# Expert slots of 160 rows in place of 128: a tail of 32 rows in float32 on four column strips

## What is computed

```python
moe = jnp.zeros_like(t)
for e in range(N_EXPERTS):          # 16
    he = jax.nn.silu(t @ w_gate[e]) * (t @ w_up[e])      # (1024, 512)
    moe = moe + gates[:, e:e + 1] * (he @ w_down[e])     # gates is 0 but for two experts a token
h = h + moe.reshape(B, S, D)
```

## Time and profile before

| | before |
|---|---|
| median of 3 runs | 1485.0 us (1484.18 to 1487.67) |
| span of the profiled execution | 1482.1 us |
| TensorE busy | 1413.0 us, 95% of the span |
| VectorE busy | 972.7 us, 66% |
| ScalarE busy | 856.3 us, 58% |
| chain that ended last | TensorE 74%, DMA 9%, VectorE 8%, ScalarE 6% |

### The profile page before, as it was taken

How to read it: one execution, slowest core, us unless ns; L and a number is a source line. 1 busy time by engine, 2 the same in 40 slices (tenths; PEclk the granted TensorE clock), 3 DMA queues, 4 the chain that set the end, 5 groups by cost and what they waited for, 6 DMA issues and landing times.

```text
span 1482.1 us, 21096 instructions
## 1 busy us (share of the span) xinstructions
PE 1413.0 (95%) x7429; PEld 1082.9 (73%) x7429; DVE 972.7 (66%) x1763; ACT 856.3 (58%) x1553; POOL 140.1 (9%) x205
## 2 busy tenths in 40 slices
PE   7999999999999999999999999978999999999996
PEld 5888999544445545468878887767788888888885
DVE  5513116367658876757763343378889899898887
ACT  6321467366656666653253333344678888878776
POOL 1000000122300200000000000001111111221211
PEclk9999999999999999999999999997999999999998
DMA  6231124420020000021120011246997666666694
GB/s 228 66 112 41 61 93 169 180 103 1 1 114 1 1 29 30 30 99 43 43 114 29 29 44 43 69 144 241 352 367 215 211 216 213 221 211 215 220 367 135
DMA packets 89397, 189.01 MB, mean 128 GB/s; under 512 B 14314, under 2 KB 24554, under 8 KB 88563
## 3 DMA queue, kind: packets, MB, share of 16 engines
q1 hardware_dynamic: 80050, 166.11, 31.5%
q0 software_dynamic: 7200, 22.03, 5.8%
q10 hardware_dynamic: 2080, 0.01, 0.1%
HBM read 218.54 MB, written 28.31 MB: 167 GB/s over the span
## 4 chain that ended last, share of the span: by engine, by line
PE 74%; DMA 9%; DVE 8%; ACT 6%; issue 3%; POOL 0%; DVEq 0%; ACTq 0%; SPq 0%; POOLq 0%
PE psum L2075 28%; PE psum L2323 17%; DMA up_stage<-in_w_up 8%; PE psum L2059 8%; PE psum L2218 7%; PE psum L2241 5%; PE psum L2200 4%; PE psum L2052 3%; DVE up_rest L1686 3%; DVE gate_rest L1686 1%; PE psum L2485 1%; ACT gate_high L1229 1%; ACT arena L1369 1%; ACT up_high L1229 1%; ACT arena L1204 1%
## 5 line engine op out<-in xcount | busy, mean ns | idle before, releaser
L898 ACT ACTIVATE arena<-psum 128x512 f32<-128x512 f32 (+3 forms) x195 | 85.7, 494 | 83.0 <-PE psum L2241 45.8
L1686 DVE TENSOR_TENSOR down_rest<-down_stage,down_high 128x1024 fp32r<-128x1024 f32 x96 | 115.0, 1219 | 25.4 <-ACT down_high L1229 25.3
L1686 DVE TENSOR_TENSOR up_rest<-up_stage,up_high 128x1024 fp32r<-128x1024 f32 x100 | 117.0, 1219 | 15.5 <-ACT up_high L1229 15.1
L2218 PE MATMUL psum<-arena 64*128 64x512 f32 (+7 forms) x384 | 115.9, 519 | 6.2 <-ACT arena L1185 4.1
L1571 DVE TENSOR_TENSOR_SCAN arena<-arena,singles 128x768 f32<-128x768 f32 (+7 forms) x64 | 86.4, 1364 | 53.7 <-POOL arena L786 47.5
L2059 PE MATMUL psum<-arena 128*128 128x512 f32 (+2 forms) x352 | 118.0, 487 | 0.8 <-DVE arena L1552 0.8
L1686 DVE TENSOR_TENSOR gate_rest<-gate_stage,gate_high 128x1024 fp32r<-128x1024 f32 x100 | 115.8, 1217 | 1.4 <-ACT gate_high L1229 1.3
L2075 PE MATMUL psum<-up_high,rows_high 128*128 128x256 f32 x384 | 110.2, 287 | 6.5 <-DVE up_rest L1686 6.1
L1229 ACT ACTIVATE up_high<-up_stage 128x1024 fp32r<-128x1024 f32 x100 | 100.3, 1056 | 23.9 <-DMA up_stage<-in_w_up 23.9
L2075 PE MATMUL psum<-up_rest,rows_high 128*128 128x256 f32 x384 | 108.6, 283 | 0.0
L2075 PE MATMUL psum<-up_high,rows_rest 128*128 128x256 f32 x384 | 108.6, 283 | 0.0
(11 more groups left out here) (417 smaller groups left out, 3535.2 us busy)
## 6 DMA issues: line engine op xcount, KB each, us to landing
gate_stage<-in_w_gate SPq DMA_DIRECT2D x25, 2048.0 KB
up_stage<-in_w_up SPq DMA_DIRECT2D x25, 2048.0 KB
down_stage<-in_w_down SPq DMA_DIRECT2D x24, 2048.0 KB
arena<-in_x SPq DMA_DIRECT2D x16, 512.0 KB, 3.7
arena<-in_w_mkv SPq DMA_DIRECT2D x8, 1024.0 KB, 6.3
arena<-in_w_in SPq DMA_DIRECT2D x4, 1024.0 KB, 10.9
arena<-in_w_mo SPq DMA_DIRECT2D x4, 1024.0 KB, 6.5
mv_times_w_mo_spill<-arena SPq DMA_DIRECT2D x8, 512.0 KB, 3.1
```

The lines of the kernel that those rows point to most:

```text
L898: do(act.activation(dst, src, ACT.Copy), s_te["act"])
L1686: ins = dve.tensor_tensor(split[part][1][:, k, :], stage[part][:, k, :], split[part][0][:, k, :].bitcast(F32), ALU.subtract)
L2218: mm = pe.matmul(scores_of(kind, n)[:, at:end], lhs, rhs(at, end), start=True, stop=True)
```

## The change

A slot now holds 160 rows of an expert: 128 as before and a **tail** of 32. The tail's rows are gathered and added on their own (`fetch_tail`, `add_tail`): the 32 rows of 1024 values are laid on 128 partitions as four pieces of 256. The tail's products are plain float32, not split, and read the weights from the stage itself. Each product of 32 rows is made four times side by side, on four strips of 32 output partitions of TensorE, each strip with another quarter of the columns (`tail_rows_by`, `tail_down`). In the queue they stand behind the main products: gate's tail behind up, up's tail behind the hidden transpositions, down's tail behind down, at the very end of the slot. Since they read the stages, `next_weights` waits for them too. Up is made in one piece of 512 columns, and the hidden values in one piece instead of two halves. The places in the table become rank + (256 - 160) x (rank // 160) + 256 x the slot.

```diff
-SLOTS = (2 * SEQ) // P + NE
+TAIL = 32
+STRIPS = P // TAIL
+ROOM = P + TAIL
+PIECE = DM // STRIPS
+SLOTS = (2 * SEQ) // ROOM + NE + 2
...
-            def next_weights(part, rests_done, e, new):
+            def next_weights(part, rests_done, tail_made, e, new):
+                if part == 1:
+                    sp.wait_ge(s_ua, tail_made)
                 sp.wait_ge(s_lo[part], rests_done)
+                if part != 1:
+                    sp.wait_ge((s_gf, s_ua, s_y)[part], tail_made)
                 load(e, part, new > 0)
...
                 fetch(idx[:, 0:1])
-                pool.wait_ge(s_yo, 2 * s + 2)
+                fetch_tail(idx[:, 2:3])
+                pool.wait_ge(s_yo, 3 * s + 2)
                 pool.sem_inc(s_go, 1)
                 add_rows()
-                pool.wait_ge(s_ya, 16 * s + 16)
+                pool.wait_ge(s_yo, 3 * s + 3)
+                pool.sem_inc(s_go, 1)
+                add_tail()
+                pool.wait_ge(s_ya, 32 * s + 32)
...
-                act.wait_ge(s_gf, s + 1)
+                act.wait_ge(s_gf, 2 * s + 1)
                 act.activation(hrow, bank(2), ACT.Silu).then_inc(s_si, 1)
+                act.wait_ge(s_xt, 3 * s + 3)
+                act.activation(xT_t, bank(4)[:, 2 * P:4 * P], ACT.Copy).then_inc(s_xh, 1)
                 high(s, 2, None)
...
-                high(s + 1, 0, s_gf)
-                high(s + 1, 1, s_ub, (0,))
+                high(s + 1, 0, None)
+                high(s + 1, 1, None, (0,))
                 act.wait_ge(s_yf, s + 1)
                 for half in range(2):
-                    act.wait_ge(s_y, 2 * s + 1 + half)
+                    act.wait_ge(s_y, 3 * s + 1 + half)
                     act.activation(ysb[:, 512 * half:512 * half + 512], bank(6 + half), ACT.Copy).then_inc(s_yo, 1)
+                act.wait_ge(s_y, 3 * s + 3)
+                act.activation(ysb_t, bank(3)[:, 0:PIECE], ACT.Copy).then_inc(s_yo, 1)
                 high(s + 1, 1, None, (1, 2, 3))
...
+            def tail_rows_by(part, dst):
+
+                for k in range(DC):
+                    at = P * (k % 2) + TAIL * (k // 2)
+                    for i in range(STRIPS):
+                        mm = pe.matmul(dst[TAIL * i:TAIL * i + TAIL, 0:P], xT_t[:, at:at + TAIL],
+                                       stage[part][:, k, P * i:P * i + P], start=(k == 0), stop=(k == DC - 1))
+                return mm
+
+            def tail_down():
+                for k in range(FC):
+                    for i in range(STRIPS):
+                        mm = pe.matmul(bank(3)[TAIL * i:TAIL * i + TAIL, 0:PIECE], hT_t[:, TAIL * k:TAIL * k + TAIL],
+                                       stage[2][:, k, PIECE * i:PIECE * i + PIECE], start=(k == 0), stop=(k == FC - 1))
+                return mm
```

More of the change, by code:

```diff
@@ L342, in moe_layer @@
         picked = cut(41440, 2 * T, NE)
+        whole_rooms = over("whole_rooms", I32, 41440, T, NE)[:, :, :]
         mark = cut(41696, 2 * T, NE)
@@ L423, in moe_layer @@
         ends_i = small("ends_i", [P, NE], I32)
-        idx_all = over("idx_all", I32, 9216, TAB, 2)
-        idx = small("idx", [P, 2], I32)
-        share = cut(9304, TAB)
+        idx_all = over("idx_all", I32, 9216, TAB, 4)
+        idx = small("idx", [P, 4], I32)
+        share = cut(9344, TAB)
+        share_t = cut(9376, TAB)
+        table_t = cut(9408, 3 * TAB)
+        pads_t = cut(9504, SLOTS)
+        piece_t = cut(9536, TAB)
+        ysb_t = cut(9600, PIECE)
+        h_t = cut(9856, P)
+        hT_t = cut(9984, P)
+        xg_t = cut(12864, PIECE)
+        xT_t = cut(13120, 2 * P)
+        onehot_t = over("tail_onehot", F32R, 13632, 2 * T, TAIL)
+        strip = small("strip", [P, 1])
+        strip_i = small("strip_i", [P, 1], I32)
         pad_row = small("pad_row", [P, 1])
@@ L735, in _ @@
             e, new = plan(1)
-            for part in range(2):
-                next_weights(part, 2, e, new)
+            next_weights(0, 2, 2, e, new)
+            next_weights(1, 2, 2, e, new)
             last = sp.snap(n_slots - 1)
@@ L740, in _ @@
                 e, new = plan(s + 1)
-                next_weights(2, 2 * s + 2, e, new)
+                next_weights(2, 2 * s + 2, 3 * s + 3, e, new)
                 e, new = plan(s + 2)
-                for part in range(2):
-                    next_weights(part, 2 * s + 4, e, new)
-            all_added = sp.snap(16 * n_slots)
+                next_weights(0, 2 * s + 4, 2 * s + 4, e, new)
+                next_weights(1, 2 * s + 4, 2 * s + 4, e, new)
+            all_added = sp.snap(32 * n_slots)
             sp.wait_ge(s_ya, all_added)
@@ L842, in _ @@
             do(pool.tensor_copy(slot_no, whole[:, 0:TAB]), s_lane)
+            do.settle()
+            do(pool.tensor_scalar(lane_t, lane[:, 0:TAIL], float(P), None, ALU.add), s_lane)
             pool.wait_ge(s_idx0, 1)
@@ L854, in fetch, with fetch_tail @@
                                         in_offset=bass.IndirectOffsetOnAxis(ap=token, axis=0)).then_inc(s_xg, 16)
+            def fetch_tail(piece):
+                pool.indirect_dma_start(out=xg_t, out_offset=None, in_=tn_dram.rearrange("s (i n) -> (s i) n", i=STRIPS),
+                                        in_offset=bass.IndirectOffsetOnAxis(ap=piece, axis=0)).then_inc(s_xgt, 16)
             def add_rows():
@@ L883, in _ @@
             pool.wait_ge(s_xg, all_fetched)
+            pool.wait_ge(s_xgt, tails_fetched)
         @block.scalar
@@ L1794, in _ @@
             dve.wait_ge(s_moeg, 16)
+            one(dve.tensor_scalar(strip_i[:, :], nums[:, NE + T:NE + T + 1], 5, None, ALU.logical_shift_right))
+            one(dve.tensor_copy(strip[:, :], strip_i[:, :]))
             def softmax_maximum(j):
@@ L2012, in _ @@
             one(dve.tensor_tensor(share, share, bank(6)[:, 2 * TAB:3 * TAB], ALU.add))
+            one(dve.tensor_tensor(share_t, table_t[:, TAB:2 * TAB], table_t[:, 2 * TAB:3 * TAB], ALU.add))
             rest(0, 1, (2, 3))
@@ L2494, in _ @@
             rows_in(0)
-            table(range(T // 2, 2 * T)).then_inc(s_tab, 1)
+            table(range(T // 2, 2 * T))
+            pe.wait_ge(s_ab, 7)
+            for c in range(2 * T):
+                mm = pe.matmul(bank(7)[0:TAIL, 0:3 * TAB], onehot_t[:, c, :], table_at[:, c, :, :].rearrange("p a s -> p (a s)"),
+                               start=(c == 0), stop=(c == 2 * T - 1))
+            mm.then_inc(s_tab, 1)
             pe.wait_ge(s_ends, 1)
```

130 lines of the change are left out of this document (80 added, 50 removed).

## The result

The changed kernel takes **1543.4 us** (median of 4 runs, 1540.2 to 1543.97) against 1485.5 for the kernel before in the same comparison: ratio 1.039, 95% interval 1.0373 to 1.0407. It is slower, as forecast, but by 3.9% where 1.1% was forecast, and it lies above the range given.

The account below looks back on a forecast made before the run. TensorE's work comes out even, so the later weight loads decide. Span 1016.75 + 28.3 + 17 x 24.5 + 15 x 1.7 + 12 = 1499.1 us, median 2.9 above: 1502 us; range 1477 to 1537, the forecast's own 1487 to 1520.

Parts of the forecast that it names:

- up is usable at U + 11.2: Up's weights usable 11.2 us after U, the issue of up's load (tail's up product end plus 0.3 us).
- the granted clock inside the loop: TensorE's clock over the expert slots: the sum had no term for a fall.
- Slots with new weights, 26.2 us: Slots that load an expert: 24.5 us of TensorE's work plus a 1.7 us wait before up, 15 times.
- TensorE's work in a slot, 24.5 us: TensorE's products and transpositions per slot: 18.5 - 0.50 + 0.33 + 6.15 = 24.5 us.
- three strip sections: Tail products for gate, up and down in each slot: 2.05 us a section, +6.15 us together.
- rival 3: Tail strips cost 0.385 us a group: 2.4 us on 18 slots, 43 us, 1545 us; chance 0.09.
- the router's 0.77 us: Cost of two router strip groups, split as 2 x 0.213 us plus 0.34 for entering and leaving the strips.
- The hidden multiply kept its cover: Multiply ready at U + 22.8, first tail section covering it until U + 23.4: 0.6 us to spare.
- Gate itself is in time: New gate weights landed at U + 4.4 and ready at U + 7.8, against TensorE's need at U + 8.5.
- The beginning and the end: Outside the loop: first gate product at 1016.75, first slot 28.3 us, end 12 us behind the last product.
- that the loads are hidden (1476): Rival for the whole loop: TensorE alone sets the pace, 1502 - 25.5 = 1476 us; chance 0.20.
- Rival 2: Down's load later than U + 17.1, hidden multiply waits: 1569 us, likelier 1535; chance 0.14.

Follow-up runs that it names:

- e5: Changed kernel with both gathers of the next rows issued only after ScalarE's first part of the new up: 1595.7 us, ratio 1.0732.
- e6: Changed kernel with ScalarE's three copies of the results moved ahead of the new up's first part: 1516.2 us, ratio 1.0199.
- e3: Changed kernel with each weight load issued as two halves of 1 MB, each with its own semaphore: 1487.2 us, ratio 1.0013.
- e4: Changed kernel with 18 transpositions of the identity put in front of up on TensorE: 1535.1 us, ratio 1.0333.
- e9: Changed kernel with only the main rows' gather held behind up's load, the tail's gather left early: 1510.1 us, ratio 1.016.
- e1: Changed kernel with every weight load after the first switched off, waits and products kept: 1472.35 us, ratio 0.9914.
- e2: Changed kernel with the tail's products cut to their first group in each section, waits and copies kept: 1504.7 us, ratio 1.0133.
- e7: Changed kernel with loads in halves and ScalarE's result copies first, together: 1492.3 us, ratio 1.0041.
- e10: Changed kernel with halves, copies first, and the add of rows held until VectorE has taken the new up's rest: 1482.7 us, ratio 0.9984.
- e12: Changed kernel with halves and the add of rows held until VectorE has taken the new up's rest, copies unmoved: 1497.9 us, ratio 1.0086.

## Why the prediction was wrong

**The mechanism was right, the size of one term was not, and one term was left out.** The steps that failed are "up is usable at U + 11.2" and the granted clock inside the loop, which the sum had at nothing. The forecast's own sum was a span of 1499.1 us; it was 1538.4, so 39.3 us are missing.

- *Slots with new weights, 26.2 us.* They took 28.2 (7 of them, 27.97 to 28.42) and 29.8 (8 of them), 435.3 us for 15 where I had 393: **+42.3**. Up, said to be usable at U + 11.2, is usable at U + 13.4. Of those 2.2 us, 1.5 are gate's load, which I had usable 6.9 us after its issue and which takes 8.4; 0.4 are its issue, 2.1 us ahead of up's and not 2.5, since the sections are shorter; 0.3 are the gathers, 1.8 for 1.5 (e5). The 6.9 came from reading by the DMA share: 0.99 over 22 us, so "busy from 1172.00 on". The stretches above show what a share hides: in the second microsecond after the issue it is 0.33 with 57 GB/s, in the third 0.91 with only 209, then 338. The kernel before had it too: in the three stretches of 1 us from 1172.00 on the rate is 86, 270 and 381 GB/s. A whole load behind no other takes 8.4 us, though 2 MB at the full rate of 400 GB/s would be 5.2. That gate shares the engines with up's load behind it, which the prediction named beside its rivals, is not the reason: gate is as fast with up 3.6 us behind it as with 2.1 (e6).
- *The granted clock*, which the sum did not have inside the loop: 8 up products of 7.34 us for 5.72, 8 x 1.6 = 13 us, part of the 42.3. I had even written the wait that caused it, 1.7 us in front of up in each slot, and had priced it as idle time only. With that wait 0.5 us longer and another of 1.3 us in front of gate, the clock fell in about every second slot; whether 1.7 us alone would have done it, no run shows (with 1.1 us in front of up, in e6, it fell once). e3, e4 and e9 give the 13 us back in three different ways. Without these 13 us the time would have been some 1530, inside the range.
- *TensorE's work in a slot, 24.5 us.* 24.43 and 24.38 in the two slots without new weights, 24.43 in all of e1. The three strip sections, 2.05 us each, took 1.88, 1.89 and 1.86. Eight groups take 1.88 us and one group 0.40 (e2), so a group is 0.21 and the fixed part 0.2, not 0.34: the 0.213 a group held, and the 0.385 a group of rival 3 is out. What the rest of the router's 0.77 us was, no run shows.
- *The other steps.* The hidden multiply kept its cover, and the copies between the first and the second part of up take 1.34 us of the chain where 1.32 were forecast. "Gate itself is in time" did not hold: TensorE waits 1.3 us in front of it. That adds nothing to the slot, since up is later still and its wait would be longer by as much; but it makes the waits of a slot 3.5 us where 1.7 were forecast.
- *The beginning and the end.* The first gate product came at 1014.58, not 1016.75: the 16 products of the tail's table took 1.28 us and not 3.2. TensorE did not wait 3 us for the tail's first rows but 0.2, so the first slot took 25.5 and not 28.3. The end took 14.2 us and not 12. Together -2.8, with -0.2 from the two light slots: 42.3 - 0.2 - 2.8 = 39.3.

The rivals: that the loads are hidden (1476) is what e1 shows for a kernel without them, 1472; it did not happen. Rival 2, down's load in front of the hidden multiply, is not in this kernel, yet it is the next one in line: it appears as soon as up is made faster (e6, e7), in e7 by the mechanism named, the add beside down, as e10 shows; in e2 it is the lost cover that brings it. The range ended at 1537, since I had widened it for rivals 2 and 3 and not for an error of 2 us in the term that is paid 15 times, nor for the clock. That the first gate product came 2.2 us early and the end took 2.2 us longer cancels by luck.

## What to carry to other kernels

When a buffer is given a second reader, its next load waits for that reader: write the closed cycle (issue, landing, conversion, product, reader, next issue) and compare it with the engine's work for one round, before counting what the engine saves. A term inside such a cycle is paid in each round, so its error is too; take the time from issue to first use of the first load in the queue, not bytes by the full rate. Splitting a load in two, so that its consumer starts on the first half, was worth more here than any single rearranging of queues (56 us against 27 and 33); a second stage for a weight, which would take the reader off the load's way altogether, was not tried. A moved transfer has to be followed to what it then stands beside and to the last round.

## What was not expected of the hardware

- A wait of 2.2 us in front of a product (and one of 1.3 us in front of another) went with a fall of TensorE's granted clock in 8 rounds of 15: 7.34 us for a product of 5.72. 18 transpositions that nobody reads, some 2 us of work, in its place made the kernel 8.3 us faster (e4).
- Float32 products on four strips of 32 output columns overlap: 32 of them with 128 columns take 1.88 us, 16 with 256 columns 1.86, and 4 alone 0.40 (e2), so 0.21 us a group of four and 0.2 for the section. One after the other, 64 records at the 0.11 us of a transposition's would be 7 us.
- A load of 2 MB with no other ahead of it needs 8.4 us from issue to use. In the first three stretches of 1 us in which its packets move, the engines' share is 0.33, 0.91 and 0.96, but the rate 57, 209 and 338 GB/s.
- The add of rows, held back, can still be moving when the next load begins: it took 49% of the engines' time for 4 us there, and the load's first half came 1.7 us later (e12).
